# A mixture-of-experts layer on one Trainium2 core: gate and up products of an expert placed side by side in quarters of the TensorE array, in 32 wider products a round in place of 64

## The reference

```python
def per_sequence(args):
    hs, cs = args
    a = jnp.einsum('sd,edf->sef', hs, w_gate)      # e: 32 experts, d: 1024, f: 256
    u = jnp.einsum('sd,edf->sef', hs, w_up)
    act = jax.nn.silu(a) * u * cs[..., None].astype(hs.dtype)
    return jnp.einsum('sef,efd->sd', act, w_down)
```

## Time and profile before

| | us |
|---|---|
| median of 3 runs | 360.4 (355.95 to 362.62) |
| time of the profiled execution | 361.69 |
| its span (first to last instruction) | 359.9 |

### The profile page before, as it was taken

One profiled execution on the slowest core, in us unless ns is written; L12 is line 12 of the kernel. 1 busy time (PEld: TensorE's weight loads), 2 busy tenths in 40 slices (PEclk: granted clock), 3 DMA queues, 4 the chain that ended last, 5 costly groups with the idle time before them and its releaser, 6 DMA issues.

```text
span 359.9 us, 11564 instructions
## 1 busy us (share of the span) xinstructions
PE 319.1 (89%) x4785; PEld 246.8 (69%) x4786; DVE 167.3 (46%) x461; ACT 121.1 (34%) x308; POOL 44.9 (12%) x79
## 2 busy tenths in 40 slices
PE   8999999999999989887799899999999949466672
PEld 6989989799875446665677677777777726446350
DVE  4478454565253612854345355555555522250433
ACT  1645056454243317432133233333333311220213
POOL 4200001353403035700000000000000000000001
PEclk9999999999999999899899999999999987998997
DMA  8999993081829999579997999999999999999953
GB/s 285 323 386 387 352 402 150 0 308 44 341 61 383 308 408 372 189 252 362 419 413 288 419 419 414 416 418 414 421 413 423 410 416 421 412 423 417 417 235 117
DMA packets 33525, 121.07 MB, mean 336 GB/s; under 512 B 5608, under 2 KB 7936, under 8 KB 26336
## 3 DMA queue, kind: packets, MB, share of 16 engines
q1 hardware_dynamic: 33312, 120.63, 85.9%
q10 hardware_dynamic: 192, 0.14, 0.1%
HBM read 119.72 MB, written 1.05 MB: 336 GB/s over the span
## 4 chain that ended last, share of the span: by engine, by line
PE 54%; SPq 29%; DMA 7%; issue 4%; ACT 2%; DVE 2%; POOLq 0%; POOL 0%; ACTq 0%; DVEq 0%
SPq L389 16%; PE bank L549 13%; SPq L401 9%; PE bank L616 7%; DMA spare<-in_w_up_dram 6%; PE bank L808 6%; PE bank L543 4%; PE bank L840 3%; SPq L383 3%; PE bank L762 3%; PE bank L563 2%; PE bank L769 2%; PE bank L525 2%; PE bank L723 1%; PE bank L578 1%
## 5 line engine op out<-in xcount | busy, mean ns | idle before, releaser
L808 PE MATMUL bank<-ring,hT 128*32 128x128 f32 x1664 | 54.6, 285 | 19.0 <-DMA ring<-in_w_up_dram 8.2
L808 PEld LDWEIGHTS bank<-ring,hT 128*32 128x32 f32 x1664 | 48.2, 115 | 28.0 <-issue 27.8
L1545 DVE SCALAR_TENSOR_TENSOR yb<-bank,pp,yb 64x512 fp32r<-64x512 f32 x34 | 25.5, 750 | 50.3 <-ACT yb L1080 49.8
L1262 DVE TENSOR_TENSOR unit_lo<-ring,unit_hi 128x2048 fp32r<-128x2048 f32 (+1 forms) x12 | 26.5, 2205 | 25.6 <-ACT unit_hi L909 25.6
L1080 ACT ACTIVATE yb<-bank,pp 64x512 fp32r<-64x512 f32 x34 | 23.2, 683 | 34.1 <-PE bank L840 33.7
L762 PEld LDWEIGHTS bank<-pp,qk 128*128 128x128 bf16 x912 | 27.9, 98 | 7.5 <-issue 5.5
L762 PE MATMUL bank<-pp,qk 128*128 128x64 bf16 x912 | 30.2, 194 | 2.9 <-issue 2.9
L616 PE MATMUL bank<-ring,qk 128*128 128x512 f32 (+1 forms) x72 | 29.9, 551 | 0.0
L1528 DVE SCALAR_TENSOR_TENSOR pp<-bank,stats,pp 128x128 f32<-128x128 f32 x18 | 6.3, 351 | 42.9 <-ACT pp L1069 42.9
L1224 POOL TENSOR_SCALAR stats<-qk 128x1 f32<-128x1 f32 x2 | 0.6, 308 | 202.1 <-ACT work L1100 202.1
L840 PE MATMUL bank<-ring,pp 128*32 128x512 f32 x208 | 25.5, 609 | 0.0
(11 more groups left out here) (217 smaller groups left out, 536.7 us busy)
## 6 DMA issues: line engine op xcount, KB each, us to landing
ring<-in_w_up_dram SPq DMA_DIRECT2D x24, 1024.0 KB, 17.1
ring<-in_w_down_dram SPq DMA_DIRECT2D x24, 1024.0 KB, 17.4
ring<-in_w_gate_dram SPq DMA_DIRECT2D x16, 1024.0 KB, 16.1
ring<-in_w_in_dram SPq DMA_DIRECT2D x5, 2048.0 KB, 19.4
ring<-in_w_gate_dram SPq DMA_DIRECT2D x16, 512.0 KB, 13.9
ring<-in_w_out_dram SPq DMA_DIRECT2D x4, 1024.0 KB, 9.3
spare<-in_w_gate_dram SPq DMA_DIRECT2D x4, 1024.0 KB, 18.9
spare<-in_w_up_dram SPq DMA_DIRECT2D x4, 1024.0 KB, 19.3
```

Source lines behind the costliest of these rows:

```text
L808: last = mm(p_gu[b:b + CAP, w * P:(w + 1) * P], hg[:, k, CAP * e:CAP * (e + 1)], w_gu[at[e]][:, w, k, h, :], start=(k == 0), stop=(k == KD ...
L1262: V.tensor_tensor(unit_lo[b][:, k, :], unit_src(u)[:, k, :], unit_hi[b][:, k, :].bitcast(fp32), ALU.subtract).then_inc(w_lo_ready, 1)
L1545: V.scalar_tensor_tensor(out=yb[half][rest, :], in0=p_y[rows, :], scalar=wcol[rows, :], in1=yb[half][rows, :].bitcast(fp32), op0=ALU.mult, ...
```

## The change

Gate and up no longer follow each other. For each k, the four quarters now hold gate of expert 0, gate of expert 1, up of expert 0, up of expert 1, each over all 256 columns: 32 products a pass. The pass waits for gate and up of both experts before its first product. `gate_half_done` and `gate_done` are gone; `gu_half_done` is raised after the first four k, `gu_done` after all. SP frees gate and up together: for places 0 and 1 half of both after `gu_half_done`, the other half after `gu_done`; for the other places all four transfers after `gu_done`. Sigmoid and the two multiplications work on 64 partitions by 256 columns, and the activation takes two transposes in place of one.

```diff
-        act_sb = pp[:, M0 + 320:M0 + 448]
-        sig, gated = pp[:, M0 + 448:M0 + 576], pp[:, M0 + 576:M0 + 704]
+        LOW, HIGH = slice(0, CP), slice(CP, 2 * CP)
+        both_sb = pp[:, M0 + 320:M0 + 320 + FE]
+        sig, act_sb, gated = both_sb[LOW, :], both_sb[LOW, :], both_sb[HIGH, :]
...
-                for w, used in enumerate((gate_done, gu_done)):
-                    if w == 0 and loads[0][1] in places(0):
-                        for part, half_used in enumerate((gate_half_done, gate_done)):
-                            sp.wait_ge(half_used, passed)
+                if loads[0][1] in places(0):
+                    for part, half_used in enumerate((gu_half_done, gu_done)):
+                        sp.wait_ge(half_used, passed)
+                        for w in range(2):
                             for e, p in loads:
-                                load_gate_part(e, p, part)
-                        continue
-                    sp.wait_ge(used, passed)
-                    for e, p in loads:
-                        load_half(e, p, w)
+                                load_part(e, p, w, part)
+                else:
+                    sp.wait_ge(gu_done, passed)
+                    for w in range(2):
+                        for e, p in loads:
+                            load_half(e, p, w)
...
-                        pe.wait_ge((gate_in, up_in)[w][at[e]], fillings * (32 if w == 0 and at == places(0) else 16))
-                    for k in range(KD):
-                        if w == 0 and k == KD // 2:
-                            pe.wait_ge(hg_ready, i + 1)
-                        for h in range(2):
-                            for e in range(2):
-                                b = CP * h + CAP * e
-                                last = mm(p_gu[b:b + CAP, w * P:(w + 1) * P], hg[:, k, CAP * e:CAP * (e + 1)], w_gu[at[e]][:, w, k, h, :],
-                                          start=(k == 0), stop=(k == KD - 1))
-                        if w == 0 and k == KD // 2 - 1:
-                            last.then_inc(gate_half_done, 1)
-                    last.then_inc((gate_done, gu_done)[w], 1)
-                    if w == 0:
+                        pe.wait_ge((gate_in, up_in)[w][at[e]], fillings * (32 if at == places(0) else 16))
+
+                for k in range(KD):
+                    if k == KD // 2:
+                        pe.wait_ge(hg_ready, i + 1)
+                    for w in range(2):
+                        for e in range(2):
+                            b = CP * w + CAP * e
+                            last = mm(p_gu[b:b + CAP, 0:FE], hg[:, k, CAP * e:CAP * (e + 1)], w_gu[at[e]][:, w, k, :],
+                                      start=(k == 0), stop=(k == KD - 1))
+                    if k == KD // 2 - 1:
+                        last.then_inc(gu_half_done, 1)
...
-                nc.tensor.transpose(p_tr[:, 2 * P:3 * P], act_sb, ident).then_inc(actt_done, 1)
+                for f in range(2):
+
+                    last = nc.tensor.transpose(p_tr[:, 2 * P + CP * f:3 * P + CP * f], both_sb[:, f * P:(f + 1) * P], ident)
+                last.then_inc(actt_done, 1)
...
-                A(sig, p_gu[:, 0:P], ACT.Sigmoid, scale=rrow).then_inc(sig_ready, 1)
+                A(sig, p_gu[LOW, 0:FE], ACT.Sigmoid, scale=rrow[LOW, :]).then_inc(sig_ready, 1)
...
-                V.scalar_tensor_tensor(out=gated, in0=p_gu[:, 0:P], scalar=rrow, in1=sig, op0=ALU.mult, op1=ALU.mult).then_inc(dve_step, 1)
+                V.scalar_tensor_tensor(out=gated, in0=p_gu[LOW, 0:FE], scalar=rrow[LOW, :], in1=sig, op0=ALU.mult, op1=ALU.mult).then_inc(dve_step, 1)
```

More of the change, by code:

```diff
@@ L254, in layer_program @@
         dn_at = [s[:, 2 * KD * FE:] for s in place] + [pp[:, 0:NT * D]]
-        w_gu = [s.rearrange("p (w k h f) -> p w k h f", w=2, k=KD, h=2) for s in gu_at]
+        w_gu = [s.rearrange("p (w k f) -> p w k f", w=2, k=KD) for s in gu_at]
         w_dn = [s.rearrange("p (h n) -> p h n", h=2) for s in dn_at]
@@ L303, in layer_program @@
         hg_half_ready, gathered_half, selo_ready = sem("hg_half_ready"), sem("gathered_half"), sem("selo_ready")
-        gate_half_done, gate_done = sem("gate_half_done"), sem("gate_done")
+        gu_half_done = sem("gu_half_done")
         hg_ready, gu_done, sig_ready, sel_ready, selw_ready = (
@@ L377, in _ @@
                 sp.dma_start(w_o[:, b // 2, b % 2], I["w_out"][0, rows, cols].rearrange("(k p) n -> p k n", p=P)).then_inc(wo_in[b], 16)
[L379 to L383, removed]
             def load_half(e, p, w):
@@ L389, in load_half, with load_part @@
                 sp.dma_start(gu[:, w, :], src.rearrange("o (p k) f -> p (o k f)", p=P)).then_inc((gate_in, up_in)[w][p], 16)
-            def load_gu(e, p):
[L393 to L398, removed]
+            def load_part(e, p, w, part):
+                gu = gu_at[p].rearrange("p (w c) -> p w c", w=2)
+                c = slice(part * KD // 2 * FE, (part + 1) * KD // 2 * FE)
+                src = I[("w_gate", "w_up")[w]][0, bass.ds(e, 1)].rearrange("o (p k) f -> p (o k f)", p=P)
+                sp.dma_start(gu[:, w, c], src[:, c]).then_inc((gate_in, up_in)[w][p], 16)
+            def load_gu(e, p):
+                for w in range(2):
+                    if p in places(0):
+                        load_part(e, p, w, 0)
+                        load_part(e, p, w, 1)
+                    else:
+                        load_half(e, p, w)
             def load_dn(e, p):
@@ L817, in one_pass @@
                         for t in range(NT):
-                            picked = mm(p_tr[:, 3 * P + 1:3 * P + 4], selo[:, t, :], rst[:, t, :], start=(t == 0), stop=(t == NT - 1))
+                            picked = mm(p_tr[:, ROWS + 1:ROWS + 4], selo[:, t, :], rst[:, t, :], start=(t == 0), stop=(t == NT - 1))
                         picked.then_inc(rr_done, 1)
+                last.then_inc(gu_done, 1)
                 pe.wait_ge(base_ready, 1)
@@ L1065, in one_pass @@
                 act.wait_ge(rr_done, i + 1)
-                A(rparts, p_tr[:, 3 * P + 1:3 * P + 4], ACT.Copy, accum_out=rrow).then_inc(rrow_ready, 1)
+                A(rparts, p_tr[:, ROWS + 1:ROWS + 4], ACT.Copy, accum_out=rrow).then_inc(rrow_ready, 1)
                 act.wait_ge(rrow_ready, i + 1)
                 act.wait_ge(gu_done, i + 1)
-                A(sig, p_gu[:, 0:P], ACT.Sigmoid, scale=rrow).then_inc(sig_ready, 1)
+                A(sig, p_gu[LOW, 0:FE], ACT.Sigmoid, scale=rrow[LOW, :]).then_inc(sig_ready, 1)
                 act.wait_ge(actt_done, i + 1)
                 nc.scalar.copy(actT, p_tr[:, 2 * P:3 * P]).then_inc(actT_ready, 1)
-                nc.scalar.copy(wcol, p_tr[:, 3 * P:3 * P + 1]).then_inc(wcol_ready, 1)
+                nc.scalar.copy(wcol, p_tr[:, ROWS:ROWS + 1]).then_inc(wcol_ready, 1)
                 act.wait_ge(added, i + 1)
```

10 lines of the change are left out of this document (7 added, 3 removed).

## The result

The changed kernel takes 361.72 us (median of 20 runs, 360.72 to 364.97) against 360.94 us before (20 runs beside them, 355.95 to 364.82): 0.8 us more, where 0.4 more was forecast, and inside the range of 357.2 to 365.6. The ratio is 1.009 (95% interval 1.0055 to 1.0125). It lies above the ratio of the two medians because it leaves out every run more than 1.5% above the fastest of its kernel, and since one run of before took 355.95 us that drops nine of its twenty, all above 361.3 us, and none of the changed kernel. The means of all runs are 362.4 and 360.7 us, so 1.7 us more (95% interval 0.5 to 2.9). By the three readings the change costs 0.8, 1.7 or 3.2 us: no gain, but a small loss, under 2% in all of them.

The account below looks back on a forecast made before the run. The prediction took the landing of the last up weights, through a full DMA queue, plus a 17.1 us tail as the bound. Terms -3.2 + 1.9 + 0.2 + 1.5 = +0.4 us gave 360.8 us, range 357.2 to 365.6.

Parts of the forecast that it names:

- What bounds the kernel: End of the span: landing of the last up weights, set by DMA engines full at 416 GB/s, plus a 17.1 us tail.
- Step 1: Gate and up products: columns set the pace, not the number of products, so about 3.8 us as before; gain 0.
- number counts: Rival: the number of products sets their time, so half of 3.8 us a pass goes; 357.6 us, chance 0.05.
- quarters overlap less: Rival: quarters overlap less well at 256 columns, a pass takes 12.5 us if they cost twice; 393 us, chance 0.04.
- Step 2: TensorE's program: 128 fewer instructions a pass, fewer late code fetches; passes 1 to 4 get back about 5 of 7.7 us.
- The rival that the idle times stay: Code comes late by the same amount or has another cause, gap 5.3 us at the release; 365.8 us, chance 0.18.
- Step 3: Freeing gate and up together: DMA queue full from the first refill on, small gap at pass 4's release; 3.2 us gained.
- Step 4: Tail: all last products wait for the ups, +1.9 us; the second transpose adds +0.2 us.
- Step 5: Sigmoid and two multiplications over 256 columns grow by 0.37 us in all, hidden by the gather; +0.4 if not.
- Step 6: Clock in the tail: a longer wait for weights brings the last products to the low clock level; +1.5 us.
- the rival that the clock holds: All of the code loss goes and the clock holds in the tail; -1.4 us, 359.0 us, chance 0.22.

Follow-up runs that it names:

- experiment 5: Changed kernel with gate and up of all places loaded, waited for and freed in two halves by k; 363.07 us, ratio 1.0089 to the kernel before.
- Experiment 3: Changed kernel with each gate and up product split in two of 128 columns, so 64 products a pass again; 366.53 us, ratio 1.0191 to before.
- experiment 6: Kernel before with every refill transfer cut to an eighth of its bytes, leaving the DMA queue nearly idle behind the first loads; 326.59 us, one run.
- experiment 1: Kernel before with only SP's waits changed, so that gate and up are freed together; 363.42 us, ratio 1.0105 to before.
- experiment 4: Changed kernel with 28 unread products ahead of the wait for weights in passes of places 6 and 7; 361.94 us, ratio 1.0022 to before.
- experiment 8: Changed kernel with gate and up loaded, waited for and freed in halves by k only in places 0, 1, 6 and 7; 361.87 us, ratio 1.0038.
- experiment 9: Changed kernel with halves by k in places 0, 1, 6 and 7, plus 18 unread products between halves in 6 and 7; 361.95 us, ratio 1.0009.
- experiment 2: Kernel before with only TensorE's waits moved: gate and up of both experts must land before the first gate product; 363.45 us, ratio 1.0109.
- experiment 12: Kernel before with 18 unread products between gate products and the wait for ups in places 6 and 7; 359.86 us, ratio 0.9991.
- experiment 10: Kernel before, unchanged, profiled once more; one profile with last ups landing 184.5 us after the start of pass 1 and a tail of 18.6 us.

## Why the prediction was right, and where it was not

- **What bounds the kernel** held: in every form with whole refills and a readable landing the chain that ends last passes through the transfer of the last ups, and from 210 to 290 us the queue moves 413 to 417 GB/s in all of them but experiment 5.
- **Step 1 (columns set the pace, gain 0)** held: 1.91 + 1.93 us for the 64 wider records, 8.74 against 8.80 us a pass without weights to wait for. The two rivals on the products (number counts; quarters overlap less) are out.
- **Step 2 (code)** held in its cause and was somewhat too careful in size. 5 of 7.7 us were to come back; the release went from 35.9 and 35.0 us (two profiles of before) to 31.2, which with the 1.95 us of later release is 6.6 and 5.8 us. Experiment 3 shows that instructions do it, the packets of the instruction queue end 1.3 to 1.5 us ahead of the products that waited, and in experiment 6 the second and third wait vanish with the full queue. The rival that the idle times stay is out. The Trainium skill's section "Instruction fetch mechanics" in "Runtime: NRT & Kernel Launch" has the blocks right; that crossing them is mostly hidden did not hold here: 3.3 to 5.3 us for three.
- **Step 3 (3.2 us gained ahead of the landing)** is the step that failed, in the size of its sum and in one term in the direction. Its part at the release held: before missed 2.7 and 1.5 us there, the changed kernel nothing (421 GB/s from 190 to 195). But the first refill was to improve from 1.7 to 0.9 us missed, and instead it went from 1.9 and 2.1 us to 2.2 and 3.6. The step took the queue as full from the first issue on, and it is not: 293, 379 and 393 GB/s in the first fifteen us. The two profiles of each kernel give a gain in the landing of 185.4 or 184.5 less 183.3 or 185.1: on the mean 0.8 us, not 3.2, and no more than the profiles of one kernel differ. A small part is the assumption that 4 KB rows are free: a twelfth of the bytes of the refills change here, a sixth of what experiment 5 changes beyond the changed kernel, so by its 2.2 us some 0.4 us (an estimate). Freeing together goes with the loss: the eight profiles of forms that do it (the changed kernel twice, experiments 1, 3, 4, 5, 8 and 9) miss 2.2 to 3.6 us in the first 20 us, the four of forms that free one by one (before twice, experiments 2 and 12) 1.5 to 2.1. Why the engines move only 250 to 300 GB/s at a share near 1 there was not tried and stays open.
- **Step 4 (+1.9 us serial, +0.2 transposes)** held: 3.9 us with the small product (experiment 4) in place of 1.95 at full clock; the second transpose 0.11.
- **Step 5 (0.37 us, hidden)** held: 468 and 477 ns in place of 368 and 351, and the transposes stand 2.01 us behind the products as before (343.79 to 345.80).
- **Step 6 (+1.5 us of clock)** held for the changed kernel (1.6 and 2.4 us in its profiles), and with it the rival that the clock holds is out. What it missed: before pays too in some executions (3.44 and 3.64 us of ups in experiments 10 and 1 in place of 1.95), so the difference is nearer 1 us.

With the terms as measured the sum is -0.8 + 1.9 + 0.1 + 1.0 = +2.2 us, near the 1.7 us of the means. Two errors, 2.4 us of gain too much in step 3 and some 0.5 us of cost too much in step 6, are each as large as the forecast of 0.4 us or larger. That it came so near the 0.8 us of the medians is luck; what the runs bear out is the range and the mechanisms of steps 1, 2, 4 and 5, and of 6 in the changed kernel.

## What to carry to other kernels

Before halving the number of products, ask whether the width or the number sets their time; a row with another width tells. If it is the width, what is left of such a change is the length of the program, and in these runs that was worth something only where code ran for the first time beside a full DMA queue. Waiting for all inputs of a stage at once cost nothing in the middle of this kernel, which the DMA queue bounds (landing 182.8 us in experiment 2), and all of it behind the last transfer, with the clock on top. And a queue that is issued to is not yet a full queue: price a refill by the GB/s of its window, not by the time of its first issue.

## What the runs showed of the hardware that was not expected

- TensorE's waits for code: three blocks of some 250 instructions cost 3.3 to 5.3 us beside a nearly full DMA queue, and only the first of them anything (1.4 us) beside short refills. TensorE goes on 1.3 to 1.5 us after the 16 KB packet has ended.
- A packet of 8192 bytes takes 314 ns and one of 4096 bytes 163 ns in the full queue; with all transfers of gate and up in rows of 4 KB it moves 410 GB/s in place of 415.
- Products that nobody reads, 3 us of them in front of a wait, kept TensorE at 2.4 GHz there (3.9 against 5.5 us).
- Pass 1 starts anywhere from 154.3 to 157.7 us in the profiles of these forms. Six records ahead of it took 2.82 us at 2.4 GHz in some and 4.29 to 4.52 us, partly at 1.2 GHz, in others; with the first it starts at 154.3 to 156.6, with the second at 155.8 to 157.7. The clock is part of the spread, and the spread is more than the whole change.
